# Delta rule inversion of a hybrid decoder trunk: both token tiles' block products issued back to back, then two projection matmuls

## The chip, the cores and the metric

The kernel runs on one core of a Trainium2 chip. The metric is the device time of one execution in microseconds (us). TensorE (PE) multiplies, with a separate weight load in front of each matmul (PEld); VectorE (DVE), ScalarE (ACT) and GpSimd (POOL) work beside it; SyncE (SP) issues the DMAs. All engines run their own program and meet at semaphores. Everything here is float32.

## The reference, cut to what matters

Two layers run over 576 tokens: a prompt of 512 and 8 samples of 8. Each layer is one wide input projection, three parallel token mixers (RG-LRU, sparse attention, gated delta rule), a gated merge and an output projection. The change touches the delta rule, which has to solve a unit lower triangular system for every chunk and head:

```
kk = jnp.einsum('nbhcd,nbhed->nbhce', kc, kc)
A = jnp.where(strict, bc[..., :, None] * kk * dmat, 0.0) + jnp.eye(C, dtype=kk.dtype)
u = lax.linalg.triangular_solve(A, bc[..., None] * vc, left_side=True, lower=True, unit_diagonal=True)
w = lax.linalg.triangular_solve(A, bc[..., None] * kc * jnp.exp(G)[..., None],
                                left_side=True, lower=True, unit_diagonal=True)
```

## The kernel before, in words

**Two kinds of PE work in one stream.** The projections are a list of units, the same for each layer, each written by the generator `dense` (its matmul is line 827) into PSUM bank 0 or 1 in turn. A unit of the input projection is 8 matmuls of 128x128 weights against 288 token columns, and ACT or DVE evicts it (ACT L1451 for the units that run out during the delta rule). I call one such matmul a dense matmul. `fill(n, end)` writes the next n dense matmuls of the stream, unless the stream has come to unit `end`. Between fills the mixers' own small products are written, so that PE has dense matmuls to do while DVE or ACT work on a small product. In the delta rule `end` is `u0 + U_MG0`, the end of the input projections that come ahead of the merge gates; how many fills have been written before decides which later fill finds nothing left.

**The delta rule.** The tokens stand in five tiles of 128 (the last one, the samples, has 64), worked through in groups (0,1), (2,3), (4). Within a group `li` is 0 or 1. After the tiles' set-up comes the inversion: 7 levels for a group of prompt tiles (sz = 1, 2, ... 64), 3 levels for the sample tile. A level has two steps, and each runs over the tiles of the group:

- the W step: for each of 4 heads and each of the two 64-row diagonal blocks, PE multiplies B by X (L1006); DVE masks the result into W (L1675, semaphore `i_wm`);
- the X step: PE multiplies Y by W (L1024) and W by Y (L1026), again in 64x64 blocks; DVE subtracts the result from X and Y (L1681, semaphore `i_xm`), which the next level's W step waits for.

At the last level of a group of prompt tiles the blocks are the whole tile: 128x128 matmuls (L1002 and L1020) stand in their place. The sample tile has one diagonal block instead of two.

Each step of each tile ends in `fill(1, ...)`, that is, one dense matmul. The order is written out by hand; DVE takes the tiles in the same order.

**Behind the delta rule** four sums of squares (L1130) are made on PE, with `fill(6, ...)` ahead of each; ACT takes their logarithm (L1565), waits for all of them, and goes on with an exponential (L1568), two gate functions (L1571, L1572) and the squares for the attention's normalization (L1577), which PE waits for at L1143.

A matmul of the source is two PE instructions in the profile, so `x2` there is one matmul, and `x16` of L1006 is one tile's W step.

Of the kernel before, what the change touches and what calls it, by code (L numbers as in the profile page):

```python
# [208 lines left out]
U_MG0, U_MG2, U_MG1, U_WO = FIRST[("mg", 0)], FIRST[("mg", 16)], FIRST[("mg", 8)], FIRST[("wo", 0)]  # L209
# [90 lines left out]
def hybrid_trunk(nc, dram, out):  # L300

    ctx = ExitStack()
    with ctx:
# [96 lines left out]
        def xy(li, n, k):  # L400

            at = XY0 + li * 2 * DN_W + k * DN_H * n
            return arena[0:n, at:at + DN_H * n].rearrange("p (h n) -> p h n", h=DN_H)
# [7 lines left out]
        def blocks(ap, sz, second):  # L411

            return ap.rearrange("p (a c) -> p a c", c=2 * sz)[:, :, second * sz:(second + 1) * sz]
# [22 lines left out]
        def diagonal(n):  # L436

            return [slice(at, at + 64) for at in range(0, n, 64)]
# [324 lines left out]
        def _(pe):  # L763
# [71 lines left out]
            def fill(n, end):  # L835

                for _ in range(n):
                    if emitted[0] < end:
                        next(stream)
# [7 lines left out]
            def step(name):  # L847

                steps_of[name] = steps_of.get(name, 0) + 1
                began[(name, steps_of[name])] = emitted[0]  # L850
# [22 lines left out]
            for l in range(DEPTH):  # L873
                past = so_far(l)
                u0 = l * N_ALL
# [68 lines left out]
                for group in DN_GROUPS:  # L944
# [48 lines left out]
                    for lev in range(levels):  # L993
                        sz = 1 << lev
                        for li, k in enumerate(group):
                            n = TILES[k][1]
                            X = xy(li, n, 0)
                            if lev:
                                pe.wait_ge(s["i_xm"], past["i_xm"] + n_ix - len(group) + li + 1)
                            for h in range(DN_H):  # L1000
                                if sz == n // 2:
                                    ins = mm(PS[0:n, 2 + li, h * P:h * P + n], tmp["B"][0:n, li, h, 0:n], X[:, h],  # L1002
                                             start=True, stop=True)
                                    continue
                                for m in diagonal(n):
                                    ins = mm(PS[m, 2 + li, h * P + m.start:h * P + m.stop], tmp["B"][m, li, h, m], X[m, h, m],  # L1006
                                             start=True, stop=True)
                            step("i_w")
                            ins.then_inc(s["i_w"], 1)
                            fill(1, u0 + U_MG0)  # L1010
                        for li, k in enumerate(group):
                            n = TILES[k][1]
                            Y, half = xy(li, n, 1), n // 2
                            pe.wait_ge(s["i_wm"], past["i_wm"] + n_iw + li + 1)
                            for h in range(DN_H):
                                w = tmp["W"][0:n, li, h, 0:n]
                                new = [PS[0:n, 4 + li, (x * DN_H + h) * half:(x * DN_H + h + 1) * half]
                                       .rearrange("p (a c) -> p a c", c=sz) for x in range(2)]
                                if sz == n // 2:
                                    ins = mm(new[1], w, blocks(Y[:, h], sz, 1), start=True, stop=True)  # L1020
                                    continue
                                if lev < levels - 1:
                                    for m in diagonal(n):
                                        mm(new[0][m], Y[m, h, m], blocks(w[m], sz, 0), start=True, stop=True)  # L1024
                                for m in diagonal(n):
                                    ins = mm(new[1][m], w[m, m], blocks(Y[m, h], sz, 1), start=True, stop=True)  # L1026
                            step("i_x")
                            ins.then_inc(s["i_x"], 1)
                            fill(1, u0 + U_MG0)
                        n_iw += len(group)  # L1030
                        n_ix += len(group)

# [1187 lines left out]
```

## Time and profile before

| | us |
|---|---|
| time, median of 3 runs (2072.47 to 2074.95) | 2072.61 |
| the profiled execution, its own time | 2070.01 |
| its span, first to last instruction | 2068.2 |
| PE busy | 1971.1 (95%) |
| DVE busy | 756.0 (37%) |
| ACT busy | 567.7 (27%) |

The profile is of one execution. A timeline merges instructions of one line that run one after the other; its first column is the start. Since the ends of matmuls are modelled and overlap the next start, durations on PE are read here from start to start. Idle time of an engine that is not the bottleneck costs nothing.

### The profile page before, as it was taken

What the parts mean: (1) busy time and instruction counts of PE and PEld (TensorE: products, weight loads), DVE (VectorE), ACT (ScalarE), POOL (GpSimd) and SP (SyncE); (2) the same over time, 40 slices, a digit from 0 to 9 for tenths busy, and PEclk for the clock granted to TensorE, in tenths of its full rate; (3) what the DMA queues carried; (4) which work ended last, traced back from release to release, by engine and by line L of the source; (5) the groups of instructions that cost most, each with busy time, mean ns of one, the idle gap of its engine ahead of it and who ended that gap; (6) DMA issues with size and microseconds to landing.
All of it is one profiled execution on the core that took longest, in us unless ns stands there. A gap on an engine that the chain in (4) does not pass through costs nothing.

```text
span 2068.2 us, 28883 instructions
## 1 busy us (share of the span) xinstructions
PE 1971.1 (95%) x11470; PEld 1408.3 (68%) x11470; DVE 756.0 (37%) x1866; ACT 567.7 (27%) x1203; POOL 80.5 (4%) x116
## 2 busy tenths in 40 slices
PE   6999899997999999999999898999979999999999
PEld 5777678785765577777467676787857555677763
DVE  2457342413444434311134663433134454433110
ACT  4132412013346511100322333120152564211000
POOL 0000201001010000000000011010101000000000
PEclk9999999998999999999999999999989999999999
DMA  6212210112411136335042141010133111553401
GB/s 233 80 61 61 66 42 21 42 47 85 132 53 31 37 99 198 107 106 166 0 162 66 41 107 41 22 42 22 47 118 120 32 31 42 154 173 103 150 39 46
DMA packets 182494, 166.78 MB, mean 81 GB/s; under 512 B 48273, under 2 KB 173635, under 8 KB 181847
## 3 DMA queue, kind: packets, MB, share of 16 engines
q1 hardware_dynamic: 178806, 147.93, 23.7%
q0 software_dynamic: 3552, 17.00, 2.2%
q8 instruction: 91, 1.49, 0.3%
q14 instruction: 45, 0.36, 0.1%
HBM read 151.44 MB, written 21.71 MB: 84 GB/s over the span
## 4 chain that ended last, share of the span: by engine, by line
PE 90%; DVE 4%; ACT 4%; issue 2%; DMA 0%; SPq 0%; ACTq 0%; DVEq 0%
PE PS L827 60%; PE PS L767 6%; PE PS L1197 2%; PE PS L1210 2%; PE PS L1006 2%; PE PS L1024 2%; PE PS L1276 1%; PE PS L1026 1%; PE PS L1266 1%; PE PS L1095 1%; PE PS L1143 1%; PE PS L936 1%; PE PS L909 1%; PE PS L1117 1%; PE PS L1350 1%
## 5 line engine op out<-in xcount | busy, mean ns | idle before, releaser
L827 PE MATMUL PS<-hT,ring 128*128 128x288 f32 x3968 | 1090.2, 416 | 29.2 <-ACT arena L1438 8.8
L827 PEld LDWEIGHTS PS<-hT,ring 128*128 128x128 f32 x3968 | 730.7, 193 | 240.6 <-issue 24.4
L827 PE MATMUL PS<-zs,owr 128*128 128x288 f32 x768 | 211.7, 409 | 0.0
L827 PEld LDWEIGHTS PS<-zs,owr 128*128 128x128 f32 x768 | 141.5, 190 | 40.5 <-issue 4.6
L767 PE MATMUL PS<-con,arena 128*128 128x128 f32 (+5 forms) x934 | 142.9, 277 | 15.6 <-DMA arena<-in_nsa_k_norm 12.2
L767 PEld LDWEIGHTS PS<-con,arena 128*128 128x128 f32 (+5 forms) x934 | 107.2, 138 | 72.8 <-issue 42.2
L827 PE MATMUL PS<-arena 128*128 128x512 f32 (+1 forms) x320 | 124.8, 593 | 2.1 <-issue 2.1
L1456 ACT ACTIVATE sg<-PS 128x288 f32<-128x288 f32 x96 | 38.8, 404 | 292.7 <-PE PS L827 292.7
L1778 DVE SCALAR_TENSOR_TENSOR mpr<-sg,PS 128x288 f32<-128x288 f32 x64 | 29.1, 454 | 208.7 <-PE PS L827 206.1
L1738 DVE SCALAR_TENSOR_TENSOR arena<-arena,par 128x512 f32<-128x512 f32 x192 | 99.5, 518 | 6.8
L827 PEld LDWEIGHTS PS<-arena 128*128 128x128 f32 (+1 forms) x320 | 52.7, 179 | 71.1 <-issue 70.9
L2075 DVE CUSTOM_DVE_ANT_0 PS<-PS,con 128x128 f32<-128x128 f32 (+3 forms) x128 | 61.9, 506 | 67.4 <-PE PS L1197 67.4
L1608 ACT ACTIVATE arena<-PS,sm 128x128 f32<-128x128 f32 (+3 forms) x128 | 66.8, 524 | 64.7 <-DVE sm L2075 58.6
L1675 DVE TENSOR_TENSOR arena<-PS,con 128x512 f32<-128x512 f32 (+3 forms) x80 | 52.7, 660 | 66.5 <-PE PS L1006 52.2
L1681 DVE TENSOR_TENSOR arena<-arena,PS 128x512 f32<-128x512 f32 (+3 forms) x70 | 43.5, 622 | 88.7 <-PE PS L1026 58.2
L1599 ACT ACTIVATE arena<-arena,sm 128x128 f32<-128x128 f32 (+3 forms) x128 | 64.6, 553 | 31.5 <-DVE sm L1675 31.5
L1451 ACT ACTIVATE zs<-PS 128x288 f32<-128x288 f32 x32 | 13.2, 411 | 173.0 <-PE PS L827 173.0
L1197 PE MATMUL PS<-arena 64*128 64x128 f32 (+3 forms) x256 | 51.8, 482 | 4.1 <-ACT arena L1608 3.9
L1024 PEld LDWEIGHTS PS<-arena 64*64 64x64 f32 x800 | 41.1, 133 | 20.0 <-issue 18.5
L1210 PE MATMUL PS<-arena 128*64 128x256 f32 x320 | 52.2, 404 | 1.4 <-DVE zs L1675 1.0
L1024 PE MATMUL PS<-arena 64*64 64x64 f32 (+1 forms) x800 | 53.5, 224 | 0.0
L1786 DVE SCALAR_TENSOR_TENSOR arena<-PS,arena 128x512 f32<-128x512 f32 x18 | 12.4, 691 | 112.0 <-PE PS L827 105.4
(291 smaller groups left out, 1872.1 us busy)
## 6 DMA issues: line engine op xcount, KB each, us to landing
ring<-in_w_in SPq DMA_DIRECT2D x54, 1024.0 KB, 5.3
arena<-in_cache_nsa_kv SPq DMA_DIRECT2D x128, 192.0 KB, 2.6
ring<-in_w_in SPq DMA_DIRECT2D x32, 256.0 KB, 3.7
arena<-in_state_nsa_win SPq DMA_DIRECT2D x32, 256.0 KB, 3.2
arena<-in_cache_nsa_kv SPq DMA_DIRECT2D x128, 64.0 KB, 1.9
arena<-in_w_out SPq DMA_DIRECT2D x4, 2048.0 KB, 10.3
out_win_sample<-in_state_nsa_win POOLq DMA_DIRECT2D x2, 4032.0 KB, 23.1
arena<-in_x_prompt SPq DMA_DIRECT2D x8, 512.0 KB, 8.6
```

The costliest lines, as they stand in the source:

```text
L767: return nc.tensor.transpose(dst, src, ident[0:src.shape[0], 0:src.shape[0]])
L827: ins = mm(to, w, x, start=start, stop=stop, skip_group_check=True)
L1006: ins = mm(PS[m, 2 + li, h * P + m.start:h * P + m.stop], tmp["B"][m, li, h, m], X[m, h, m], start=True, stop=True)
L1024: mm(new[0][m], Y[m, h, m], blocks(w[m], sz, 0), start=True, stop=True)
L1197: mm(PS[:, 4 + g, 0:q0 + P], qk7[m, r, q0:q0 + P], qk7[m, 5 + br, 0:q0 + P], start=True, stop=True).then_inc(s["a_s"], 1)
L1210: ins = mm(PS[g * HD:(g + 1) * HD, 7, rp * 2 * P:(rp + 1) * 2 * P], ktok[:, kb, col:col + HD], pTring[j % 2][:, g * 2 * P:(g + 1) * 2 * P] ...
L1599: A(p, p, ACT.Copy, scale=sm8[:, 7, u % 8:u % 8 + 1]).then_inc(s["a_n"], 1)
L1608: A(pring[slot % PRING][:, 0:width], PS[:, 4 + slot % 2, 0:width], ACT.Exp, scale=-1.0, bias=sm8[:, 0, k:k + 1], accum_out=sm8[:, 1, k:k + ...
L1675: return V.tensor_tensor(dst, a, b, ALU.mult)
L1681: return V.tensor_tensor(dst, a, b, ALU.subtract)
L1738: ins = stt(out=d, in0=e, scalar=w(j), in1=d, op0=ALU.mult, op1=ALU.add)
L2075: V.tensor_tensor_reduce(out=raw, in0=raw, in1=C("causal")[:, 3 * P - q0:4 * P], scale=-1.0, scalar=-NEG, op0=ALU.add, op1=ALU.min, accum_ ...
```

## The change

In both steps of a level the fill moves out of the loop over the tiles and becomes `fill(2, ...)`:

```
@@ -1007,7 +1007,7 @@
                                              start=True, stop=True)
                             step("i_w")
                             ins.then_inc(s["i_w"], 1)
-                            fill(1, u0 + U_MG0)
+                        fill(2, u0 + U_MG0)
                         for li, k in enumerate(group):
                             n = TILES[k][1]
                             Y, half = xy(li, n, 1), n // 2
@@ -1026,7 +1026,7 @@
                                     ins = mm(new[1][m], w[m, m], blocks(Y[m, h], sz, 1), start=True, stop=True)
                             step("i_x")
                             ins.then_inc(s["i_x"], 1)
-                            fill(1, u0 + U_MG0)
+                        fill(2, u0 + U_MG0)
                         n_iw += len(group)
                         n_ix += len(group)
```

For a group of two tiles the number of dense matmuls stays at two per step. The sample tile is alone in its group, so its six steps (3 levels, two each) get two dense matmuls in place of one.

PE's order where the inversion of the first group begins, before (here x8 counts matmuls of the source):

```order
L827 MATMUL PS<-hT,ring 128x288 x3
L1006 MATMUL PS<-arena 64x64 x8
L827 MATMUL PS<-hT,ring 128x288
L1006 MATMUL PS<-arena 64x64 x8
L827 MATMUL PS<-hT,ring 128x288
L1024 MATMUL PS<-arena 64x64 x2
```

and with the change:

```order
L827 MATMUL PS<-hT,ring 128x288 x3
L1006 MATMUL PS<-arena 64x64 x16
L827 MATMUL PS<-hT,ring 128x288 x2
L1024 MATMUL PS<-arena 64x64 x2
L1026 MATMUL PS<-arena 64x64 x2
L1024 MATMUL PS<-arena 64x64 x2
```

The dense matmul that stood between the two tiles' blocks now stands behind both. The X step changes in the same way.

PE's order behind the delta rule of the first layer, where the dense matmuls ahead of the merge gates run out (L1117 is the delta rule's last product, L1130 the sums of squares, L1143 the attention's):

```order
 L1117 MATMUL PS<-arena 128x512 x2
 L827 MATMUL PS<-hT,ring 128x288 x10
-L1130 MATMUL PS<-arena,con 128x288 x2
-L827 MATMUL PS<-hT,ring 128x288 x6
-L1130 MATMUL PS<-arena,con 128x288 x6
+L1130 MATMUL PS<-arena,con 128x288 x8
 L1143 MATMUL PS<-arena,con 128x288 x2
 L827 MATMUL PS<-hT,ring 128x288 x3
```

The six dense matmuls that the sample tile's steps take in addition are the six that stood between the first and the second of the four sums.

ACT's order at the same place (L1451 evicts a dense unit, L1561 makes squares, L1565 the logarithms):

```order
 L1561 ACTIVATE arena<-arena 128x576 x4
-L1451 ACTIVATE zs<-PS 128x288 x3
+L1451 ACTIVATE zs<-PS 128x288 x4
 L1565 ACT_TABLE_LOAD
-L1565 ACTIVATE arena<-PS,con 128x576
-L1451 ACTIVATE zs<-PS 128x288
-L1565 ACTIVATE arena<-PS,con 128x576 x3
+L1565 ACTIVATE arena<-PS,con 128x576 x4
 L1568 ACT_TABLE_LOAD
```

The last unit is now evicted ahead of the table load and of the first logarithm. DVE, POOL and SP keep their order.

## Rows read from the trace of the kernel before

**Rows 1.** Page, part 4: shares of the span of the chain that ended last

```profile
PE 90%; DVE 4%; ACT 4%; issue 2%; DMA 0%; SPq 0%; ACTq 0%; DVEq 0%
```

**Rows 2.** Timeline of PE, one level of the first group: start us, us, instructions

```profile
272.69 0.68 PE L1006 MATMUL PS<-arena 64*64 64x64 f32 x16
273.30 0.75 PE L827 MATMUL PS<-hT,ring 128*128 128x288 f32 x2
273.99 0.68 PE L1006 MATMUL PS<-arena 64*64 64x64 f32 x16
274.60 0.75 PE L827 MATMUL PS<-hT,ring 128*128 128x288 f32 x2
275.28 0.33 PE L1024 MATMUL PS<-arena 64*64 64x64 f32 x4
...
276.36 0.75 PE L827 MATMUL PS<-hT,ring 128*128 128x288 f32 x2
...
278.12 0.75 PE L827 MATMUL PS<-hT,ring 128*128 128x288 f32 x2
278.80 0.68 PE L1006 MATMUL PS<-arena 64*64 64x64 f32 x16
```

**Rows 3.** Timeline of the weight loads in the same level; bracket: idle before, releaser

```profile
273.98 0.54 PEld L1006 LDWEIGHTS PS<-arena 64*64 64x64 f32 x16 [0.39 <-issue]
```

**Rows 4.** Timeline of PE, last level of that group and the work behind it

```profile
308.67 0.75 PE L827 MATMUL PS<-hT,ring 128*128 128x288 f32 x2
309.26 1.05 PE L1002 MATMUL PS<-arena 128*128 128x128 f32 x8
...
316.50 2.10 PE L827 MATMUL PS<-hT,ring 128*128 128x288 f32 x8
318.44 1.89 PE L1038 MATMUL PS<-arena 128*128 128x256 f32 x8
```

**Rows 5.** Line L1006 by itself, all places: idle before its weight loads (us, times)

```profile
  issue: 19.3, 50
  DVE arena L1681: 1.5, 4
```

**Rows 6.** Timeline of DVE in that level; bracket: idle before, releaser

```profile
273.49 0.69 DVE L1675 TENSOR_TENSOR arena<-PS,con 128x512 f32<-128x512 f32 x1 [3.32 <-PE PS L1006]
...
276.48 0.69 DVE L1681 TENSOR_TENSOR arena<-arena,PS 128x512 f32<-128x512 f32 x1 [1.07 <-PE PS L1026]
```

**Rows 7.** Timeline of PE, first steps of the sample tile

```profile
445.49 0.67 PE L1006 MATMUL PS<-arena 64*64 64x64 f32 x8
446.10 0.75 PE L827 MATMUL PS<-hT,ring 128*128 128x288 f32 x2
446.78 0.30 PE L1024 MATMUL PS<-arena 64*64 64x32 f32 x2
```

**Rows 8.** Timeline of PE behind the delta rule of the first layer

```profile
497.72 3.07 PE L827 MATMUL PS<-hT,ring 128*128 128x288 f32 x12
500.63 3.27 PE L1130 MATMUL PS<-arena,con 128*128 128x288 f32 x12
515.03 2.29 PE L1143 MATMUL PS<-arena,con 128*128 128x288 f32 x4 [11.13 <-ACT arena L1577]
```

**Rows 9.** Timeline of ACT at the same place

```profile
496.41 1.28 ACT L1565 ACT_TABLE_LOAD   x1
...
500.83 0.41 ACT L1451 ACTIVATE zs<-PS 128x288 f32<-128x288 f32 x1 [2.17 <-PE PS L827]
501.80 0.74 ACT L1565 ACTIVATE arena<-PS,con 128x576 f32<-128x576 f32 x1 [0.56 <-PE PS L1130]
...
503.93 0.74 ACT L1565 ACTIVATE arena<-PS,con 128x576 f32<-128x576 f32 x1 [0.42 <-PE PS L1130]
...
514.29 4.12 ACT L1577 ACTIVATE arena<-arena 128x576 f32<-128x576 f32 x7 [0.74 <-DVE zs L1675]
```

**Rows 10.** Stretches: busy PE, PEld, DVE, ACT, POOL; granted PE clock; DMA share, GB/s

```profile
272.69:308.67 35.98, 35.98 (x623) 25.49 (x622) 15.87 (x23) 1.23 (x3) 0.00 (x0) 1.00 0.10 32
...
458.04:468.39 10.35, 10.35 (x65) 10.35 (x64) 0.00 (x0) 0.41 (x1) 0.00 (x0) 0.67 0.00 0
468.39:472.06 3.67, 3.67 (x9) 2.62 (x10) 0.42 (x1) 0.00 (x0) 3.35 (x2) 0.54 0.00 0
```

More of the change, by code:

```diff
@@ L1009, in _ @@
                             ins.then_inc(s["i_w"], 1)
-                            fill(1, u0 + U_MG0)
+                        fill(2, u0 + U_MG0)
                         for li, k in enumerate(group):
@@ L1028, in _ @@
                             ins.then_inc(s["i_x"], 1)
-                            fill(1, u0 + U_MG0)
+                        fill(2, u0 + U_MG0)
                         n_iw += len(group)
```

## The prediction, made before the changed kernel ran

> **What bounds the kernel now.** I read the chain of work that ended last first: PE carries 90% of the span [rows 1], so time taken off PE's stream comes off the end unless another engine is late. Then PE's timeline through one level of the inversion, from start to start [rows 2]. PE never stands still there, yet its pace is uneven. The W step is 0.61 (tile 0's 16 block instructions), 0.69 (one dense matmul), 0.61, 0.68: 2.59 us. The X step is 1.08 (32 block instructions), 0.68, 1.08, 0.68: 3.52 us. A level takes 6.11 us. The weight loader, which runs ahead of PE elsewhere, stands idle 0.39 us ahead of each run of blocks, and no semaphore releases it ("issue") [rows 3]. That happens at nearly every one of the 54 runs of L1006 [rows 5]. It is not the wait on DVE that the code has there: that row is of the very first level, whose W step of tile 1 waits for nothing.
>
> **What an edge between the two kinds of work costs.** In an undisturbed row four dense matmuls take 318.44 - 316.50 = 1.94 us [rows 4], 0.485 each. The one between two runs of blocks takes 0.68 [rows 2]; the one between blocks and a full-size L1002 takes 0.59 [rows 4]. So a dense matmul that has blocks on both sides pays 0.20 us more. The blocks pay too: 16 instructions take 0.61 and 32 take 1.08, that is 0.0294 each and 0.14 left over per run [rows 2]. One dense matmul set between two runs of blocks thus costs 0.34 us above the work itself.
>
> The Trainium skill gives this a name (TensorEngine Tiling (Array Packing), Key Properties): changing the tiling mode drains the engine, changing the tile within a mode does not. By that rule the seam between tile 0's and tile 1's blocks is free, which is what I take below; no row of before shows that seam. Another of its rules speaks against the change (TensorE: Matmul & The Clock Gate, the step on LDWEIGHTS): the engine pulls weight loads ahead of running matmuls, by which an edge would cost nothing, the change would save nothing, and only the small loss computed further down would remain, some 2074 us. The idle 0.39 us of the loader denies it for this edge.
>
> **Part 1, the groups of two tiles.** New W step: 32 block instructions in one run, 1.08 as the X step's run of 32 shows; then two dense matmuls, 0.68 + 0.485 = 1.17: 2.25 us in place of 2.59. New X step: 64 in one run, 2 x 1.08 - 0.14 = 2.02, then 1.17: 3.19 in place of 3.52. A level falls from 6.11 to 5.43 us, 0.68 less. There are 2 groups x 6 levels with blocks x 2 layers = 24 such levels: 16.3 us. The seventh level has full-size matmuls, which have no such edge behind a dense matmul (0.59 against 0.68 is already the edge ahead of it) [rows 4]; I take nothing there, at most some 0.1 us per group either way.
>
> **Does DVE keep up?** The only thing that PE waits for in a level is DVE. DVE begins W's mask 0.80 us after the run of blocks starts (272.69 to 273.49), and X's subtraction 1.20 us after (275.28 to 276.48), each 0.69 us long [rows 2, 6]. Set out from the new W step at 0: blocks of tile 1 from 0.47, dense from 1.08, X step of tile 0 from 2.25, of tile 1 from 3.2, next level at 5.43. The mask of tile 0 is done at 1.49, wanted at 2.25: 0.76 us of slack. The mask of tile 1 is done at 2.18, wanted at 3.2. The subtractions are done at 4.14 and 5.1, wanted at 5.43 and 5.9. The tightest slack today is 275.28 - (273.49 + 0.69) = 1.10 us, so it shrinks to about 0.76; a hand-over takes about 0.15 (the first of seven squares of ACT, 0.59 each, ends at 514.88, and PE starts at 515.03) [rows 8, 9]. So no new wait. The fills' own eviction wait is on a unit finished eight dense matmuls ago, and stays as it is.
>
> **Part 2, the sample tile.** Its six steps get one more dense matmul each: 6 x 0.485 = 2.91 us more per layer, with no new edge, since each already has one [rows 7]. The same six vanish between the sums of squares, where they take 500.63 - 497.72 = 2.91 us [rows 8]. PE's sum is nil. But they covered something there: ACT's table load (1.28 us at 496.41) ran beside them, and it has to come behind the last eviction [rows 9]. Let T be the time at which the last dense matmul is through. Before, the first sum (0.97 for two matmuls) lies ahead of the run-out, so 500.63 is T + 0.97, and the last logarithm ends at 503.93 + 0.74 = 504.67, T + 5.01. With the change: eviction from T + 0.20 to 0.61, table load to 1.91, first logarithm to 2.65, while its sum was ready at T + 1.17. PE's third sum waits for that first logarithm (the banks alternate): 2.65 + 0.15 = 2.80; its logarithm starts 1.17 later (500.63 to 501.80) [rows 8, 9]; the fourth sum starts at 3.77, its logarithm at 4.94, and ends at T + 5.68. That is 0.67 us later. Behind it stands ACT's chain up to L1577, for which PE waits 11.13 us idle [rows 8], so all of it counts: 0.7 per layer, 1.3 us in all. Bounds: 0 if the table load overlaps, 1.3 per layer if all of it is laid bare.
>
> **Sum.** -16.3 + 1.3 = -15.0 us. Against the profiled execution: 2070.0 - 15.0 = 2055.0 (its span 2068.2 to 2053.2). The median of the runs stands 2.6 us above that execution, so I forecast 2072.6 - 15.0 = 2057.6 us.
>
> **The clock.** Both inversions run at a granted clock of 1.00, the 2.4 GHz level, though more than half of their time is blocks. The one place nearby where the clock falls is the 10.35 us of 128x16 products at 458.04, mean 0.67; the four dense matmuls behind it take 3.67 in place of 1.94 us [rows 10]. The change shifts such places in time, and the low stretch behind each may end earlier or later, a us or two either way; that widens the range.
>
> **Rivals.**
> - *Only the dense side gains.* If the seam between the tiles' blocks still costs the 0.14 (the tiles write different banks, and no row shows the seam), each step saves 0.20: 48 steps, 9.7 us, with the 1.3 of part 2 a time of 2064.2. For it: nothing beyond the missing row. Against it: L1024 and L1026 alternate inside a run with no visible gap. Chance 0.12.
> - *DVE turns into the bound of each step.* It has 0.76 us of slack; it decides only once hand-overs take more than that, against 0.15 seen. A wait of 0.3 per step would return 14 us and end at 2072. Chance 0.04.
> - *Slower: the clock falls inside the inversions.* The longest run without a dense matmul doubles from 1.08 to 2.02 us. If PE were brought down to 1.2 GHz by it and held there, each of the 4 dense matmuls of 24 levels would take 0.485 us more, 47 us: 2057.6 + 47, some 2104; it decides against the change once a third of the levels is hit. Against it: the share of dense work in a level rises, and the fall at 458 came only in a run of 10 us. Chance 0.04.
> - *The change doesn't do what it says* would need the dense stream to have run out in the inversions; its matmuls run on behind them [rows 8], so it has not.
>
> **How the numbers follow.** Forecast case 0.80, with its own range from 2053.5 to 2061 (part 2's bounds, the clock's ends, the spread of the median of before). The range of 8 in 10 takes in the first rival: 2052.5 to 2065. A measurement of this kernel can tell about 0.2%, 4 us, from no change. Faster: 0.80 + 0.12 and a little of the DVE case, 0.93. Same: the rest of that case and a clock that falls only now and then, 0.03. Slower: 0.04.
>
> **What would show it.** In the changed profile one level takes 5.43 us, with 1.08 from the first L1006 to the dense row and 1.17 from there to L1024, and some 2.0 for the X step's run; the loader's 0.39 us gap appears 24 times fewer at L1006. The clock of the inversions stays at 1.00. DVE's idle times are all ended by PE. L1130 runs as one row, and the wait at L1143 stays near 11 to 12.5 us. I am wrong if the run of 32 takes 1.22, if PE waits for L1675 or L1681, or if the clock column leaves 1.00.

## The result

| | median, us | runs |
|---|---|---|
| before | 2073.26 | 4, 2072.47 to 2074.95 |
| changed | 2053.69 | 4, 2053.18 to 2055.89 |

The ratio is 0.9903, 95% interval 0.9889 to 0.9918: faster by 19.6 us, where 15.0 had been forecast. The profiled execution of the changed kernel took 2055.89 us with a span of 2054.1 us, its slowest of the four.

**A level of the inversion.** The timeline of PE through one level of the first group, in the changed kernel (it answers to [rows 2]; columns as there):

```profile
299.89 1.15 PE L1006 MATMUL PS<-arena 64*64 64x64 f32 x32
300.96 1.24 PE L827 MATMUL PS<-hT,ring 128*128 128x288 f32 x4
302.13 0.33 PE L1024 MATMUL PS<-arena 64*64 64x64 f32 x4
302.30 0.28 PE L1026 MATMUL PS<-arena 64*64 64x64 f32 x4
...
304.14 1.24 PE L827 MATMUL PS<-hT,ring 128*128 128x288 f32 x4
```

The next level's L1006 starts at 305.31. From start to start: 1.07 us for the 32 block instructions, 1.17 for two dense matmuls, 2.01 for the X step's 64, 1.17 again: 5.42 us, where the level took 6.11. There is no trace of an edge between the two tiles' blocks. The granted clock is 1.00 from the layer's first L1006 up to L1095 (columns as in [rows 10]); it is the same in the second layer:

```profile
278.18:335.66 57.48, 57.48 (x762) 47.50 (x762) 21.31 (x35) 5.86 (x12) 0.00 (x0) 1.00 0.09 26
335.66:458.22 122.56, 122.52 (x1185) 100.90 (x1184) 38.34 (x80) 23.53 (x68) 7.96 (x12) 1.00 0.16 43
```

**DVE in that level** (it answers to [rows 6]):

```profile
300.62 1.29 DVE L1675 TENSOR_TENSOR arena<-PS,con 128x512 f32<-128x512 f32 x2 [1.09 <-PE PS L1006]
303.33 0.69 DVE L1681 TENSOR_TENSOR arena<-arena,PS 128x512 f32<-128x512 f32 x1 [1.42 <-PE PS L1026]
304.26 0.69 DVE L1681 TENSOR_TENSOR arena<-arena,PS 128x512 f32<-128x512 f32 x1 [0.25 <-PE PS L1026]
```

Both masks are through at 301.91, before tile 0's X step starts (302.13), and both subtractions at 304.95, before the next W step (305.31). DVE's idle times are all ended by PE: it waits, nobody waits for it. L1006 by itself (it answers to [rows 5]) still shows 0.39 us of idle loader ahead of a run, in 30 places and not in 54:

```profile
  DVE arena L1681: 7.7, 20
  issue: 3.9, 10
```

Most of these are now put down to DVE, because its semaphore came shortly before. The idle time is the same 0.39 us as where nothing was waited for, so the name says nothing here.

**Behind the delta rule of the first layer**, PE (it answers to [rows 8]), and ACT (to [rows 9]):

```profile
490.36 5.12 PE L827 MATMUL PS<-hT,ring 128*128 128x288 f32 x20
495.31 2.10 PE L1130 MATMUL PS<-arena,con 128*128 128x288 f32 x8
498.12 2.18 PE L1130 MATMUL PS<-arena,con 128*128 128x288 f32 x8 [0.71 <-ACT arena L1565]
511.44 2.29 PE L1143 MATMUL PS<-arena,con 128*128 128x288 f32 x4 [11.14 <-ACT arena L1577]
```

```profile
495.51 0.41 ACT L1451 ACTIVATE zs<-PS 128x288 f32<-128x288 f32 x1 [3.47 <-PE PS L827]
495.94 1.28 ACT L1565 ACT_TABLE_LOAD   x1
497.24 1.37 ACT L1565 ACTIVATE arena<-PS,con 128x576 f32<-128x576 f32 x2
499.37 0.74 ACT L1565 ACTIVATE arena<-PS,con 128x576 f32<-128x576 f32 x1 [0.76 <-PE PS L1130]
500.34 0.74 ACT L1565 ACTIVATE arena<-PS,con 128x576 f32<-128x576 f32 x1 [0.23 <-PE PS L1130]
```

The table load lies bare between the last eviction and the first logarithm, and the third sum waits 0.71 us for that logarithm, as part 2 of the prediction had worked out. (Its list of signs says that L1130 runs as one row; that sign did not come, and it did not fit part 2.) The last logarithm ends at 501.08, 5.77 us after the last dense matmul (forecast 5.68). The wait at L1143 is 11.14 us, as long as before.

**Where the 19.6 us are.** The table sets the first start of a line against the first start of the next one, in each layer (both layers agree within 0.1 us but for the last row). It needs no durations.

| stretch, per layer | before | changed | forecast | measured |
|---|---|---|---|---|
| L1006 to L1038: inversion, group (0,1) | 42.08 | 37.97 | -4.08 | -4.11 |
| L1066 to L1095: inversion, group (2,3), and sample tile | 123.76 | 122.56 | -4.08 + 2.91 = -1.17 | -1.20 |
| L1095 to L1108: the 128x16 products and four dense matmuls | 16.50 | 14.88 | 0 | -1.62 |
| L1130 to L1143: sums of squares, ACT's chain | 18.28 | 16.13 | -2.91 + 0.67 = -2.24 | -2.15 |
| L1143 to L1197: the attention's normalization | 65.1 | 64.6, 64.4 | 0 | -0.5, -0.7 |

Two layers make -19.3, and the stretches ahead of the second layer's L1006 another -0.3. The two profiled executions are only 14.1 us apart, because the head of the program, which the change does not touch, happened to take 5.5 us more: the first L1006 starts at 272.69 in the one and at 278.18 in the other.

So the inversions and ACT's chain gave what was forecast: 14.9 of 15.0 us. Of the other 4.7 us, 3.2 are the 1.6 us per layer at L1095, and they are TensorE's clock. The 1.2 us behind L1143 go with shorter low stretches as well: before, the granted clock is 0.50 (1.2 GHz) for the first 4.5 and 4.6 us from the start of L1143, changed for the first 3.6 and 3.3 us. What made the last 0.3 us was not looked into. The stretches from L1095 to L1108, before and changed, first layer (columns as in [rows 10]; the granted clock is the figure behind the five engines' busy times, 0.69 and 0.77):

```profile
458.04:474.54 16.50, 16.50 (x86) 14.74 (x84) 1.10 (x2) 0.41 (x1) 5.83 (x4) 0.69 0.00 0
```

```profile
458.22:473.10 14.88, 14.88 (x85) 12.88 (x83) 1.10 (x2) 0.41 (x1) 6.19 (x4) 0.77 0.21 62
```

PE is busy throughout in both, with the same instructions. A mean granted clock of 0.69 is 10.2 us of 16.5 at 1.2 GHz, 0.77 is 6.8 us of 14.88.

### The profile page after: what moved, and what is told of

It reads as the page before. It is cut to its first block, busy times and chain, and to the rows that moved or that the text cites. A ratio compares the mean times of both kernels' runs of the same rounds, so it can differ in the third digit from the quotient of the medians.

```text
span 2054.1 us, 28883 instructions
## 1 busy us (share of the span) xinstructions
PE 1954.8 (95%) x11470; PEld 1407.2 (69%) x11470; DVE 754.0 (37%) x1866; ACT 567.1 (28%) x1203; POOL 80.6 (4%) x116
## 4 chain that ended last, share of the span: by engine, by line
PE 90%; DVE 4%; ACT 4%; issue 1%; DMA 0%; SPq 0%; ACTq 0%; DVEq 0%
PE PS L827 60%; PE PS L767 6%; PE PS L1197 2%; PE PS L1210 2%; PE PS L1006 1%; PE PS L1276 1%; PE PS L1024 1%; PE PS L1026 1%; PE PS L1266 1%; PE PS L1095 1%; PE PS L1143 1%; PE PS L1156 1%; PE PS L936 1%; PE PS L909 1%; PE PS L1117 1%
## 5 line engine op out<-in xcount | busy, mean ns | idle before, releaser
L827 PE MATMUL PS<-hT,ring 128*128 128x288 f32 x3968 | 1077.9, 416 | 29.2 <-ACT arena L1438 8.8
L767 PE MATMUL PS<-con,arena 128*128 128x128 f32 (+5 forms) x934 | 143.6, 278 | 16.4 <-DMA arena<-in_nsa_k_norm 13.9
L1599 ACT ACTIVATE arena<-arena,sm 128x128 f32<-128x128 f32 (+3 forms) x128 | 64.6, 553 | 31.6 <-DVE sm L1675 31.6
L1451 ACT ACTIVATE zs<-PS 128x288 f32<-128x288 f32 x32 | 13.1, 410 | 164.3 <-PE PS L827 164.3
L1197 PE MATMUL PS<-arena 64*128 64x128 f32 (+3 forms) x256 | 51.8, 482 | 4.2 <-ACT arena L1608 3.9
L1026 PE MATMUL PS<-arena 64*64 64x64 f32 (+1 forms) x816 | 51.2, 218 | 0.0
L1024 PE MATMUL PS<-arena 64*64 64x64 f32 (+1 forms) x800 | 51.2, 221 | 0.0
```

Of the source, the lines that this page charges most:

```text
L767: return nc.tensor.transpose(dst, src, ident[0:src.shape[0], 0:src.shape[0]])
L827: ins = mm(to, w, x, start=start, stop=stop, skip_group_check=True)
L1197: mm(PS[:, 4 + g, 0:q0 + P], qk7[m, r, q0:q0 + P], qk7[m, 5 + br, 0:q0 + P], start=True, stop=True).then_inc(s["a_s"], 1)
L1599: A(p, p, ACT.Copy, scale=sm8[:, 7, u % 8:u % 8 + 1]).then_inc(s["a_n"], 1)
```

## The experiments

Two theories stood for the forecast part: an edge between dense and 64x64 work costs 0.34 us wherever it is, and DVE's chain is the next bound behind it. For the unforecast part there were two more: **A**, where the low stretches of the clock fall is a matter of time (in the first expectations: of the execution; later: of when their place in the program comes), or **B**, the additional dense matmuls of the sample tile shorten them. Beside the medians below, the kernel before took 2073.24 us with the first four, 2073.30 with the next four and 2072.93 with the last two.

**The changed kernel once more.** 

> The changed kernel once more, unedited. In the first pair of profiles the stretch from the first 128x16 product (L1095) to the next transpose (L1108) was 1.6 us shorter than before in both layers, since PE stood at 1.2 GHz for 6.8 us there and not for 10.2. Theory A (where the low stretch falls depends on the execution): the stretch is longer or shorter in this profile, 14.9 or 16.5 us, while the time stays near 2053.7 us. Theory B (the change itself shortened it): 14.9 us again in both layers. The inversions: 4.11 us less per group of two tiles than before, in both theories.

Measured: 2054.24 us (2052.53 to 2056.44), ratio 0.9911 (0.9894 to 0.9927). The stretch:

```profile
455.11:469.98 14.87, 14.87 (x85) 13.00 (x83) 1.10 (x2) 0.41 (x1) 6.00 (x4) 0.77 0.21 59
```

The low stretch has the same length at the same place, in both layers, though this execution's head was 3.1 us shorter (first L1006 at 275.08). Between these two profiled executions it does not vary, so A in its first form falls for this kernel. The inversions: 37.97 us again.

**Pairs only.**

```
                             step("i_w")
                             ins.then_inc(s["i_w"], 1)
-                            fill(1, u0 + U_MG0)
+                        fill(len(group), u0 + U_MG0)
...
                             step("i_x")
                             ins.then_inc(s["i_x"], 1)
-                            fill(1, u0 + U_MG0)
+                        fill(len(group), u0 + U_MG0)
```

> Two dense matmuls per step for the groups of two tiles as in the changed kernel, but one per step for the sample tile as before. The inversions save 4 x 4.11 = 16.4 us as in the changed kernel, and the sums of squares keep six dense matmuls between the first and the second, so that ACT's table load stays hidden: 1.5 us (2 x 0.76) faster than the changed kernel at that place, and L1130 doesn't wait for L1565. If the shorter low stretch at L1095 is owed to the sample tile's extra dense matmuls (theory B), this kernel loses 3.2 us there and ends at 2055.4 us; if it isn't (theory A), 2052.2 us.

Measured: 2058.62 us (2057.25 to 2060.05), ratio 0.9928 (0.9912 to 0.9945), slower than both theories had it. The inversion of group (0,1) took 37.97 us, and the sums kept their 18.28 us. But two low stretches of the clock came where the changed kernel has one, the first right behind the sample tile's inversion, on the four dense matmuls ahead of L1095:

```profile
449.69 3.90 PE L827 MATMUL PS<-hT,ring 128*128 128x288 f32 x8
453.42 10.67 PE L1095 MATMUL PS<-arena 128*128 128x16 f32 x64
463.93 3.68 PE L827 MATMUL PS<-hT,ring 128*128 128x288 f32 x8
```

These four dense matmuls take 3.73 us, where a run of four takes 1.94. L1066 to L1095 is 121.34 us; 122.56 - 2.91 = 119.65 was due. And L1095 to L1108 is back at 16.50. Together 3.3 us per layer are lost to the clock, against 0.76 us per layer gained at the sums. Two layers make 5.1 us; by the medians the kernel is 4.4 us slower than the changed one (2054.24).

**Sample tile only.**

```
-                            fill(1, u0 + U_MG0)
+                            fill(3 - len(group), u0 + U_MG0)
```

(in both steps.) 

> The groups of two tiles as before, two dense matmuls per step for the sample tile alone. No edge is removed, so the inversions save nothing. Theory A: 1.5 us slower than before (ACT's table load laid bare twice, 0.76 us each), 2074.8 us. Theory B (the extra dense matmuls shorten the low stretch at L1095 by 1.6 us per layer): 1.7 us faster than before, 2071.6 us.

Measured: 2073.33 us (2071.98 to 2076.84), ratio 1.0002 (0.9992 to 1.0011). The inversions save nothing (42.08), as an edge theory wants it. L1066 to L1095 is 126.68, 2.92 more than before, and the sums give back 2.16: the bare table load costs 0.76. L1095 to L1108 takes 16.51 us, so the additional dense matmuls do not shorten the low stretch by themselves: B falls, by the profile. The time alone does not decide between the two forecasts. The 1.5 us that should then be lost are within what a run can tell; in the profile 0.34 and 0.42 us of them come back between L1143 and L1156.

**The W step only.**

```
                             step("i_w")
                             ins.then_inc(s["i_w"], 1)
-                            fill(1, u0 + U_MG0)
+                        fill(len(group), u0 + U_MG0)
```

> Only the W step's two fills are put behind both tiles; the X step keeps one behind each tile; the sample tile as before. If each removed edge between dense and 64x64 work is worth 0.34 us whatever stands around it, a level takes 5.77 us (W step 2.25, X step 3.52) and the kernel 24 x 0.34 = 8.2 us less than before, 2065.1 us. Rival, that the gain needs the longer distance to DVE which merging both steps gives: well under half of the gain, 2067 us or more. Rival, that only the weight loads of L1006 were late: nearly the whole gain, 2058 us.

Measured: 2065.78 us (2064.55 to 2068.42), ratio 0.9963 (0.9948 to 0.9977). The first group's inversion takes 40.03 us, 2.05 less than before, that is 0.34 per level, and half of the changed kernel's 4.11. An edge costs the same ahead of L1006 as ahead of L1024, and the gain adds up. Both rivals fall, the second by the time as well, the first (2067 us or more) by the profile alone, since single runs reach 2068.42 us.

**All dense matmuls behind the X step.** From the changed kernel:

```
-                        fill(2, u0 + U_MG0)
+                        fill(0 if len(group) == 2 else 2, u0 + U_MG0)
...
-                        fill(2, u0 + U_MG0)
+                        fill(4 if len(group) == 2 else 2, u0 + U_MG0)
```

> From the changed kernel: in the groups of two tiles no dense matmul behind the W step and four behind the X step; the sample tile as in the changed kernel. It takes away one more edge per level (0.34 us) and with it all cover between W and X. If DVE's chain counts as in the working of the prediction, tile 0's X step can start only at 0.80 + 0.69 + 0.15 = 1.64 us after W's start, and a level takes 1.64 + 2.02 + 0.68 + 3 x 0.485 = 5.80 us, 0.37 more than the changed kernel's 5.43: 24 levels, 8.8 us, 2062.7 us, and the profile shows PE waiting for L1675. If only the number of edges counts, a level takes 5.09 us and the kernel 2045.7 us.

Measured: 2066.31 us (2065.46 to 2067.49), ratio 0.9967 (0.9955 to 0.998). PE's timeline through a level:

```profile
275.61 1.15 PE L1006 MATMUL PS<-arena 64*64 64x64 f32 x32
277.16 0.33 PE L1024 MATMUL PS<-arena 64*64 64x64 f32 x4 [0.40 <-DVE arena L1675]
...
279.17 2.21 PE L827 MATMUL PS<-hT,ring 128*128 128x288 f32 x8
```

and its line in the list of waits (us in total, times, longest):

```profile
PE PS L1024 <- DVE arena L1675: 8.1, 24, 0.4
```

Now PE waits for the mask in every level. This level, the first, takes 281.31 - 275.61 = 5.70 us, 0.27 more than the changed kernel's, and the ones behind it 5.62 or 5.63: one edge fewer, and yet slower. X starts 1.55 us behind W, where 1.64 had been worked out; DVE's first mask (276.41 + 0.69) was through 0.06 us before PE went on, so the hand-over of 0.15 had been set too high. In the next level DVE begins earlier too, 0.73 us behind W (281.31 to 282.04), and X starts 1.47 us behind it. The missing edge also saved only the 0.20 us of a dense matmul: the X step's run of 64 still takes 279.17 - 277.16 = 2.01 us, with its 0.14 us left over, though it now starts behind a wait. Per group that is 1.42 us, 5.7 in all, and not 8.8. The other half of the loss is again the clock, with the same instructions:

```profile
458.48:476.64 18.16, 18.16 (x86) 15.95 (x84) 1.10 (x2) 0.41 (x1) 6.79 (x4) 0.62 0.19 58
```

18.16 us where the changed kernel takes 14.88: 3.3 us per layer, 6.5 in all. 5.7 + 6.5 = 12.2 us is the whole distance to the changed kernel (12.1 to its second measurement).

**Three dense matmuls moved ahead of the sample tile's inversion**, once from the pairs-only kernel and once from the changed one. They are missing later, between the first two sums in the one and ahead of the sums in the other:

```
+                    if len(group) == 1:
+                        fill(3, u0 + U_MG0)
                     last_k = group[-1]
```

> As e1_pairs_only, with three dense matmuls more right ahead of the sample tile's inversion (they are missing later, between the first two sums of squares). It moves the sample tile's inversion and L1095 1.46 us later and changes nothing in them. e1 showed the clock at 1.2 GHz for 3.4 us late in that inversion (1.7 us lost per layer) and for 10.2 us around L1095. Theory A (what counts is where these places fall in time): the low stretch in the inversion goes away or moves, and the kernel ends 3 us or more below e1, some 2055 us. Theory B (one dense matmul per step is too little for the sample tile once the pairs are merged): it stays, 1066 to 1095 takes 122.8 us as e1's 121.34 plus 1.46, and the time stays at 2058.6 us.

Measured: 2056.18 us (2055.73 to 2057.37), ratio 0.9921 (0.9905 to 0.9938). L1066 to L1095 takes 121.10 us: the 119.65 that were due before, plus 1.46. The low stretch ahead of L1095 is gone (granted clock of the stretch from the sample tile's set-up to L1095):

```profile
436.00:452.93 16.93, 16.93 (x122) 12.61 (x121) 2.79 (x7) 4.03 (x15) 0.00 (x0) 1.00 0.02 8
```

against pairs only:

```profile
436.00:453.42 17.42, 17.42 (x117) 12.73 (x115) 2.78 (x7) 3.88 (x14) 0.00 (x0) 0.90 0.03 11
```

The low stretch went as A had it, but the whole fell by 2.4 us and not by 3 or more, and it isn't this stretch alone: from L1143 to L1156 a layer takes 0.8 to 0.9 us more than with pairs only, from L1156 to L1197 1.7 us less, and between the layers 2.4 us were added.

> The changed kernel with the same three dense matmuls more right ahead of the sample tile's inversion. Theory A (where the places fall decides): the low stretch at L1095 goes back from 6.8 to 10.2 us or moves otherwise, the stretch from L1095 to L1108 differs from 14.88 us in both layers, and the time differs from 2054 us by 2 us or more. Theory B (the doubled dense matmuls of the sample tile shorten it): 14.88 us again, 2054 us.

Measured: 2059.83 us (2058.03 to 2060.9), ratio 0.9939 (0.9922 to 0.9955): 5.6 us slower than the changed kernel, by an edit that adds no work.

```profile
455.92:472.44 16.52, 16.52 (x86) 14.41 (x84) 1.10 (x2) 0.51 (x2) 6.45 (x4) 0.69 0.21 63
```

L1095 to L1108 is at 16.52 again in both layers, 1.64 more each; L1143 to L1156 takes 25.00 and 24.93 in place of 24.20; the inversions stay at 37.97. The doubled dense matmuls are still there, all work around L1095 is the same, and the clock differs: B falls once more. Cut where the clock falls, the changed kernel's stretch (two rows) and this one's (two rows) read:

```profile
458.22:463.86 5.64, 5.64 (x53) 5.64 (x51) 0.00 (x0) 0.00 (x0) 0.00 (x0) 1.00 0.00 0
463.86:470.69 6.83, 6.83 (x24) 5.53 (x24) 0.42 (x1) 0.41 (x1) 3.78 (x3) 0.50 0.09 10
455.92:460.04 4.12, 4.12 (x39) 4.12 (x37) 0.00 (x0) 0.13 (x1) 0.00 (x0) 1.00 0.81 243
460.04:470.28 10.24, 10.24 (x39) 8.84 (x39) 0.42 (x1) 0.00 (x0) 4.29 (x3) 0.50 0.01 5
```

In both profiles of the changed kernel and in this one, in both layers, the clock falls 185.4 to 185.7 us after the layer's first L1006. L1095 starts 180.0 us after it there and 181.5 us here, so that less of the run lies ahead of the fall, and the low stretch lasts longer. That fits A in its second form, and it shows why a head of another length changes nothing: the fall keeps its distance from the first L1006. Why it does, and what ends a low stretch, is not shown; nor is it excluded that the three dense matmuls ahead of the inversion count by what they are, and not only by the time that they take.

**Dense matmuls behind the sums of squares.** From the changed kernel:

```
                             step("b_pe")
                             ins.then_inc(s["b_pe"], 1)
-                            fill(4, u0 + U_MG0)
+                            fill(3, u0 + U_MG0)
...
                 for n in range(DN_H):
-                    fill(6, u0 + U_MG0)
                     pe.wait_ge(s["sq_ok"], past["sq_ok"] + SQ["o"] + n + 1)
```

> From the changed kernel: three in place of four dense matmuls behind each of the four L1117 products, and none ahead of the sums of squares (L1130), so that ten dense matmuls run behind the sums, while ACT makes the logarithms and the exponential, and not ahead of them. PE stood idle there for 11.1 us waiting for L1577. The sums start 4.85 us earlier (10 x 0.485), or some 4.5 us if VectorE's last state update holds them, and ACT's chain with them; the last eviction then comes about 0.5 us behind the exponential. Expected: 4 us less per layer, 2046 us; if the chain to L1577 is bound elsewhere, 2054 us again.

Measured: 2045.8 us (2045.36 to 2047.46), ratio 0.9872 (0.9855 to 0.9888), 8.4 us under the changed kernel. PE's timeline (a line was taken out, so the sums are L1129 here and L1142 stands for L1143):

```profile
487.49 4.24 PE L1129 MATMUL PS<-arena,con 128*128 128x288 f32 x16
491.56 5.01 PE L827 MATMUL PS<-hT,ring 128*128 128x288 f32 x20
503.94 2.29 PE L1142 MATMUL PS<-arena,con 128*128 128x288 f32 x4 [7.37 <-ACT arena L1576]
```

The ten dense matmuls now run in what was an idle wait, which falls from 11.14 to 7.37 us. L1108 to the sums takes 17.36 us and not 22.21 (4.85 less, as worked out), and 0.33 come back in ACT's chain, where the last eviction is late. The low stretch at L1095 is as long as in the changed kernel (14.87).

**Breaking up the small products.** From that kernel, with one dense matmul behind each head of L1095 (8 matmuls of the source, that is 16 of the run's 64 instructions), or one behind every four matmuls of the source; two in place of four dense matmuls behind the run:

```
                                 ins = mm(PS[:, 3, at:at + 2 * DEC_SEQ].rearrange("p (x t) -> p x t", x=2), S0[:, b, h, :],
                                          w_and_q(h, b), start=True, stop=False, skip_group_check=True)
+                            fill(1, u0 + U_MG0)
                         step("b_pe")
                         ins.then_inc(s["b_pe"], 1)
-                        fill(4, u0 + U_MG0)
+                        fill(2, u0 + U_MG0)
```

> From e6: inside the run of 64 products of 128x16 (L1095, 32 matmuls of the source) one dense matmul behind each of the four heads, and two in place of four behind the run; the two more are missing behind the sums of squares, where they cost nothing. If the run of small products is what brings PE to 1.2 GHz (6.8 us low per layer in e6, half of it lost), a run broken up every 8 matmuls may keep the 2.4 GHz level: L1095 to L1108 then takes 14.88 + 0.97 - 3.4 = 12.5 us, and the kernel 2039 us. If a fall of the same length comes all the same: 15.9 us and 2046 us; anything between means a shorter low stretch.

Measured: 2052.29 us (2051.53 to 2054.46), ratio 0.99 (0.9884 to 0.9917), 6.5 us slower than the kernel that it was made from. L1095 to L1108, first layer (17.51 in the second as well):

```profile
457.87:475.38 17.51, 17.51 (x90) 15.09 (x88) 1.10 (x2) 0.41 (x1) 5.97 (x4) 0.71 0.20 60
```

The clock fell all the same, and for 10.2 us; the four executions had nearly the same mean clock, 0.978 or 0.979. The second version has this inside the loop over the products in place of the fill behind each head:

```
+                                if b % 4 == 3:
+                                    fill(1, u0 + U_MG0)
```

> As e8, with one dense matmul behind every four products of L1095 (eight in the run). If the clock falls for want of dense work in the run, this one holds it more surely than e8: L1095 to L1108 takes 14.4 us without a low stretch. Six dense matmuls fewer than in e6 are left behind the sums, which start 2.9 us later while the last eviction no longer holds ACT (1.1 us): 1.8 us per layer given back, some 2043 us. If the clock falls in both, 2049 us.

Measured: 2045.26 us (2044.09 to 2051.58), ratio 0.9866 (0.9849 to 0.9882), level with the kernel that it was made from. In the profile L1095 to L1108 takes 17.81 us, six dense matmuls (2.91 us) above the 14.87, with the low stretch still 6.8 us long. But the profiled execution was the slowest, 2051.58 us at a mean granted clock of 0.980, and the other three took 2044.09 to 2045.42 us at 0.985 or 0.986: an estimate from these figures, (0.985 - 0.980) x 2 x 2045, is some 20 us less at 1.2 GHz. Without the two low stretches at L1095 the profiled time would be 2051.6 - 6.8 = 2044.8 us, which is where the three lie; but no profile shows which stretches they lacked. One dense matmul behind each head did not keep the clock up. Whether two did, in three executions of four, stays open.

## Why the prediction was right, point by point

**Right: PE bounds it, and the edges are the gain.** The edge of 0.34 us per pair (0.20 on the dense matmul, 0.14 on the blocks) was read from before alone. 24 levels at 0.68 made 16.3 us; measured 4 x 4.11 = 16.4. With W alone it is half (2.05 of 4.11 per group). That it takes 64x64 work to make an edge, and not any change between two lines, the trace of before shows in the seventh level, where a dense matmul stands between two full-size runs and takes 310.64 - 310.15 = 0.49 us, as in an undisturbed row:

```profile
310.15 0.65 PE L827 MATMUL PS<-hT,ring 128*128 128x288 f32 x2
310.64 1.05 PE L1002 MATMUL PS<-arena 128*128 128x128 f32 x8
```

The rule of the Trainium skill (TensorEngine Tiling (Array Packing), Key Properties), by which only a change of tiling mode drains the engine, agrees: the seam between two tiles' blocks is free (1.07 us for 32 instructions). The other rule of the Trainium skill that was weighed, that weight loads are pulled ahead of running matmuls (TensorE: Matmul & The Clock Gate, the step on LDWEIGHTS), does not reach over such an edge: the loader's 0.39 us of idle time stays wherever an edge stays. What the engine does inside at an edge no row shows; the rows show the price.

**Right: DVE keeps up, with the slack shown.** The experiment without cover behind W puts DVE on the path at once and costs 0.27 us in the first level of a group and 0.20 in the others. The working was 0.09 us too careful in the first level (its hand-over of 0.15 measured 0.06) and 0.17 in the others, where DVE also begins earlier. Also, DVE's second mask follows the first after 0.60 us and not 0.69, so that both are done even earlier than set out.

**Right: the sample tile moves work without a gain, and lays ACT's table load bare.** Forecast 0.67 us per layer, measured 0.76 (2.91 - 2.15).

**Mis-sized: the clock.** The prediction put "a us or two either way" into the range and nothing into the sum. The stretches at L1095 gave 3.2 us and those behind L1143 another 1.2, 4.4 us in all, and that is all but 0.2 of the distance between the 15.0 us forecast and the 19.6 measured. (The forecast time, 2057.6 us, lies only 3.9 above the measured 2053.7, because the median of before moved from 2072.61 to 2073.26.) The prediction looked at the low stretch at L1095 alone as "the one place nearby"; the one behind the wait at L1143 stood in the trace of before too, with a granted clock of 0.55 from 515.00 to 520.00. That the sign was a gain is luck. It could not be read from the rows, and the same kernel with three dense matmuls moved gives all of it back (2059.83 us). Yet it isn't chance from one execution to the next either: both profiles of the changed kernel have the same low stretches at L1095, in both layers.

**The rivals.** The one with a costly seam between tiles needed the run of 32 at 1.22 us; it is 1.07. A DVE bound did not come, nor a low clock within the inversions of the pairs: L1006 to L1038 is 37.97 us in every kernel with both steps merged and two dense matmuls behind each, and the granted clock is 1.00 there. Behind the sample tile's inversion it did come, in the pairs-only kernel, which no rival had.

## What to carry to other kernels

Where small tiled matmuls are interleaved with full-size ones as cover, count the changes between the two kinds and not only the matmuls: here each run of dense work set between 64x64 work cost 0.34 us, and grouping the small work of two independent tiles removed half of them, while DVE still had time enough behind each step. Go on merging only as far as the consumer's latency allows, since with the last cover gone one edge fewer was slower. Cover is best placed where the engine would stand idle: ten dense matmuls moved behind the sums of squares brought another 8 us.

## What the runs showed of the hardware that was not expected

- An edit that only shifts work by 1.46 us moved the kernel by +5.6 us in one case and by -2.4 us in the other, by way of the granted clock. Low stretches of 6.8, 10.2 or 13.7 us came at one and the same place (L1095) in kernels with the same instructions there, and the same length came back when the changed kernel was profiled again. Four executions of the last kernel lie 2044.09 to 2051.58 us apart, with mean granted clocks of 0.986 to 0.980. Differences of a few microseconds between variants of this kernel say little about the edit until the clock of each stretch has been compared, in more than one execution.
- The products of 128x16 go at the pace of the clock. Before, 3.46 us of their run were at the upper level and all 64 instructions took 468.39 - 458.04 = 10.35 us [rows 10]; in the changed kernel it was 5.64 us, and they took 466.59 - 458.22 = 8.37. An estimate from either, with time at 1.2 GHz counted half, is 6.9 or 7.0 us for the run at 2.4 GHz. PE counted as fully busy in both:

```profile
458.22 8.53 PE L1095 MATMUL PS<-arena 128*128 128x16 f32 x64
466.59 4.19 PE L827 MATMUL PS<-hT,ring 128*128 128x288 f32 x8
```
